# Sixteen conditioning pieces in eight buffers instead of four, and the first squares ahead of the turns

## The chip, the cores and the metric

The kernel runs on one core of a Trainium2 chip. The metric is the device time of one execution in microseconds (us), the median of several runs.

## The reference

One layer of a decoder trunk, for a prompt of 1024 tokens and 8 single-token samples (1032 columns in all, 1024 features), in float32. What matters here is its opening:

```python
mod = jax.nn.silu(c) @ w_ada + b_ada                 # 9 rows of c, w_ada is 1024 x 6144
sh1, sc1, gt1, sh2, sc2, gt2 = jnp.split(mod[:, None, :], 6, axis=-1)
h = rmsnorm(x, norm1_g) * (1.0 + sc1) + sh1
proj = h @ w_in                                      # then conv, RG-LRU, mLSTM and pooling on its parts
x = x + gt1 * (mix @ w_out)
h2 = rmsnorm(x, norm2_g) * (1.0 + sc2) + sh2
x = x + gt2 * (jnp.square(jax.nn.relu(h2 @ w_ff1)) @ w_ff2)
```

`mod` is the conditioning. The normalised `h` of feature tile k needs tile k of `sh1` and of `sc1`, so eight column pairs of `w_ada` must have been worked through before all of `h` is there.

## The kernel before

Activations lie feature-major: 8 tiles of 128 features, 1032 tokens cut into three chunks of 344. Each dense product is made of three matmuls per tile (high by high, low by high, high by low part), so every operand is first split: ScalarE copies it to the high part (`H_hi`, `W_hi`), GpSimd or VectorE subtracts that from the whole (`H_lo`, `W_lo`).

One list, `MIX_ORDER` (line 93), is the order of the first half of the kernel. Each of the engines walks over the whole list and takes the words that concern it, in this order, and waits on semaphores in between; nothing overtakes on an engine. The words of the opening:

- `ADA:i:h`: half h of conditioning pair i (two column tiles of `w_ada`, one piece of 512 KB). TensorE: 8 matmuls (line 2383). ScalarE, for h = 1: copies the result to the one tile ADS (line 1298), when the turn before has been made.
- `ADT:i`: TensorE turns ADS (4 matmuls, line 2397) into a bank that `ADM:i` must have freed. `ADM:i`: VectorE adds the bias and writes MOD (lines 1718, 1720).
- `SQ:c:p`: squares of four tiles of chunk c on ScalarE (line 1279), added up on VectorE (line 1764), two buffers between them. `NS:c`: TensorE spreads the sums over the partitions (line 2403), ScalarE takes the root (line 1258), VectorE the reciprocal (line 1743).
- `N:c:k`: VectorE normalises tile k (lines 1729, 1733), ScalarE adds the shift and makes the high part (lines 1240, 1252, 1253), GpSimd the low part (line 1086). It needs the pairs k // 2 (shift) and 4 + k // 2 (scale), hence `ADA_START = (0, 4, 1, 5, 2, 6, 3, 7)`.
- `W:u`: the split of the weights of unit u, from WR for the first three, high part on ScalarE (line 1235), low part on VectorE for the first two (line 1778). `DK:u:c:a:b`: matmuls of unit u, chunk c, for the tiles a to b, on TensorE (lines 2412 to 2414); it waits for `W:u`'s low part and for each tile's low part.
- `WV:j`: split of V's weights, `WV_hi` on ScalarE and `WV_lo` on VectorE (line 1782); `V:t`: V for 128 tokens (lines 2439 to 2441). It needs all of `WV_lo`.
- `R:n`: ScalarE issues the load of piece n of the later ones.

The pieces are loaded into the four buffers of `RAWW` (`RAW = 4`), piece n into n modulo 4. SyncE issues the first twenty (line 810): it waits (`raw_used`, line 562) until TensorE has used piece n - 4. After some of them it issues other loads (`SP_AFTER`, line 67): W0's weights after piece 5, W1's after piece 7, V's weights and the second chunk of X after piece 15. V's weights take the place of the residual X, which isn't used until much later: `WV_raw` in front, `WV_lo` behind it; `WV_lo` is first written when all sixteen first pieces have been used.

Of the kernel before, what the change touches and what calls it, by code (L numbers as in the profile page):

```python
# [149 lines left out]
D:10:2 HM:1 R:49 R:48 LD:4 EX:2 W:12  # L150
D:11:0 SMB:1 S:2 SX:2 AB:2 NU:2 ADT:18 U:2 CN:2 ADM:18 HN:2 R:50
D:11:1 SMB:2 HM:2 R:52 EX:3 ADA:19:0 S:3 SX:3
D:11:2 SMB:3 AB:3 ADA:19:1 W:13 LDO:0 R:51 NU:3
D:12:0 ADT:19 U:3 HN:3 HM:3 R:53 CN:3 ADM:19 LD:5 ADA:20:0 EX:4 R:55
D:12:1 S:4 SX:4 ADA:20:1 Y:0 R:54 SMC AB:4 NU:4
D:12:2 R:56 U:4 ADT:20 HN:4 W:14 YD:0 R:58 HM:4 LD:6
D:13:0 Y:1 ADM:20 CN:4 ADA:21:0 EX:5 YD:1 R:57
# [129 lines left out]


def build(nc, I, O):
    plan, raw_seq = plan_mix()  # L290
# [23 lines left out]
    with ExitStack() as ctx:  # L314
# [236 lines left out]
        def load_raw(e, n):
            key = raw_seq[n]
            if key[0] == "ADA":
                w = AH * P
                e.dma_start(RAWW[:, n % RAW, :].rearrange("p (e n) -> p e n", e=2),
                            I["WADA"][2 * key[1]:2 * key[1] + 2, :, key[2] * w:(key[2] + 1) * w].rearrange("e p n -> p e n")
                            ).then_inc(raw_in[n % RAW], 16)
# [2333 lines left out]
```

## Time and profile before

| | us |
|---|---|
| median of 3 runs | 1172.3 (1172.24 to 1173.58) |
| profiled execution | 1172.33 |
| its span, first to last instruction | 1170.5 |
| TensorE busy | 1123.7 |
| VectorE, ScalarE, GpSimd busy | 795.6, 470.4, 341.7 |

Times are in us from the start of the span. A row of the timeline gives the start, the time until its last instruction ends, the engine, the line and the operation; in brackets stands the idle time ahead of it and who ended it. "SPq" is SyncE's queue: the time that an issue took, not the transfer. Busy times of TensorE are modelled. PEclk is the clock that was granted to TensorE as a share of 2.4 GHz.

### The profile page before, as it was taken

How to read it: one execution, taken by the hardware profiler on the slowest of the kernel's cores; microseconds unless marked ns; L12 is line 12 of the kernel's file. 1: busy time of each engine (PE TensorE's matmuls, PEld its weight loads, DVE VectorE, ACT ScalarE, POOL GpSimd, SP SyncE). 2: the span in 40 equal slices, each digit the busy share in tenths (PEclk: the TensorE clock that was granted, in tenths of full speed). 3: DMA queues.
4: the chain of work that ended last, by engine and by line, in shares of the span. 5: the costliest groups of instructions: out<-in, count | busy, mean ns of one | idle time of the engine just before them, and what ended most of it. 6: DMA issues, size and time to landing. Idle time of an engine off the chain costs nothing.

```text
span 1170.5 us, 19691 instructions
## 1 busy us (share of the span) xinstructions
PE 1123.7 (96%) x7237; PEld 1075.4 (92%) x7237; DVE 795.6 (68%) x1327; ACT 470.4 (40%) x774; POOL 341.7 (29%) x273
## 2 busy tenths in 40 slices
PE   4899999999989999999999999999999999999997
PEld 2688888888978999899999999999999999999996
DVE  4472455489775434778678879778778787788546
ACT  5452355555456343642233332332432433433431
POOL 1133011201425357764022032122231231231352
PEclk9799999999989999999999999999999999999998
DMA  9812523566623822111111111202202102111104
GB/s 316 311 66 82 142 91 126 171 186 225 187 79 122 270 75 72 54 55 37 37 36 55 56 36 60 66 18 72 67 9 80 59 18 78 47 53 55 37 1 145
DMA packets 67846, 109.85 MB, mean 94 GB/s; under 512 B 6435, under 2 KB 42567, under 8 KB 67399
## 3 DMA queue, kind: packets, MB, share of 16 engines
q1 hardware_dynamic: 57574, 84.88, 21.9%
q10 hardware_dynamic: 10208, 24.12, 6.5%
q8 instruction: 41, 0.67, 0.2%
q14 instruction: 23, 0.18, 0.0%
HBM read 96.81 MB, written 12.18 MB: 93 GB/s over the span
## 4 chain that ended last, share of the span: by engine, by line
PE 81%; DVE 11%; ACT 3%; issue 1%; POOL 1%; DMA 1%; SPq 0%; ACTq 0%; POOLq 0%; DVEq 0%
PE D L2412 7%; PE D L2414 6%; PE D L2413 6%; PE D L2596 6%; PE D L2598 5%; PE D L2597 5%; PE X L2598 5%; PE X L2596 5%; PE X L2597 5%; PE X L2668 5%; PE X L2670 5%; PE X L2669 5%; PE D L2668 2%; PE D L2670 2%; PE D L2669 2%
## 5 line engine op out<-in xcount | busy, mean ns | idle before, releaser
L2412 PE MATMUL D<-H_hi,W_hi 128*128 128x344 f32 x472 | 159.1, 337 | 6.9 <-POOL H_lo L1086 6.1
L2414 PE MATMUL D<-H_hi,W_lo 128*128 128x344 f32 x472 | 152.1, 322 | 0.0
L2413 PE MATMUL D<-H_lo,W_hi 128*128 128x344 f32 x472 | 152.1, 322 | 0.0
L1086 POOL TENSOR_TENSOR Y_lo<-FU,Y_hi 128x344 fp32r<-128x344 f32 (+3 forms) x84 | 100.1, 1195 | 153.7 <-ACT Y_hi L1522 87.6
L1081 POOL TENSOR_TENSOR W_lo<-RAWW,W_hi 128x1024 fp32r<-128x1024 f32 x25 | 61.3, 2452 | 178.8 <-ACT W_hi L1235 178.5
L2412 PEld LDWEIGHTS D<-H_hi,W_hi 128*128 128x128 f32 x472 | 90.1, 191 | 17.7 <-issue 11.8
L1086 POOL TENSOR_TENSOR Y_lo<-EY,Y_hi 128x344 fp32r<-128x344 f32 (+1 forms) x24 | 38.3, 1597 | 216.3 <-ACT Y_hi L1522 144.5
L2413 PEld LDWEIGHTS D<-H_lo,W_hi 128*128 128x128 f32 x472 | 90.1, 191 | 0.6 <-issue 0.2
L2414 PEld LDWEIGHTS D<-H_hi,W_lo 128*128 128x128 f32 x472 | 89.8, 190 | 0.0
L2220 DVE SCALAR_TENSOR_TENSOR X<-X,MOD 128x344 f32<-128x344 f32 (+1 forms) x138 | 75.6, 566 | 9.3 <-PE X L2670 9.2
L2668 PE MATMUL X<-Y_hi,W_hi 128*128 128x344 f32 x252 | 80.7, 320 | 0.0
L2669 PE MATMUL X<-Y_lo,W_hi 128*128 128x344 f32 x252 | 80.6, 320 | 0.0
L2670 PE MATMUL X<-Y_hi,W_lo 128*128 128x344 f32 x252 | 80.5, 319 | 0.0
L2022 DVE SCALAR_TENSOR_TENSOR X<-D,MOD,X 128x344 f32<-128x344 f32 (+1 forms) x72 | 41.3, 573 | 45.5 <-PE D L2598 24.7
L2412 PE MATMUL D<-Y_hi,W_hi 128*128 128x344 f32 x192 | 62.0, 323 | 1.5 <-POOL W_lo L1081 1.5
L1098 POOL TENSOR_TENSOR SS<-SS,SQ 128x344 f32<-128x344 f32 x45 | 43.4, 964 | 65.8 <-ACT SQ L1431 40.5
L1086 POOL TENSOR_TENSOR Y_lo<-KEPT,Y_hi 128x344 fp32r<-128x344 f32 x24 | 26.3, 1097 | 121.5 <-ACT Y_hi L1522 121.5
L2414 PE MATMUL D<-Y_hi,W_lo 128*128 128x344 f32 x192 | 61.3, 320 | 0.0
L2413 PE MATMUL D<-Y_lo,W_hi 128*128 128x344 f32 x192 | 61.3, 319 | 0.0
L1557 ACT ACTIVATE W_hi<-RAWW 128x1024 fp32r<-128x1024 f32 x30 | 31.7, 1058 | 63.9 <-PE X L2670 55.3
L1086 POOL TENSOR_TENSOR H_lo<-FU,H_hi 128x344 fp32r<-128x344 f32 (+2 forms) x33 | 29.6, 916 | 71.4 <-ACT FU L1253 57.8
L2670 PEld LDWEIGHTS X<-Y_hi,W_lo 128*128 128x128 f32 x252 | 47.4, 188 | 0.0
(417 smaller groups left out, 3434.8 us busy)
## 6 DMA issues: line engine op xcount, KB each, us to landing
RAWW<-in_W SPq DMA_DIRECT2D x76, 512.0 KB, 3.6
RAWW<-in_WADA ACTq DMA_DIRECT2D x28, 512.0 KB, 4.1
RAWW<-in_WADA SPq DMA_DIRECT2D x20, 512.0 KB, 6.5
RAWW<-in_W ACTq DMA_DIRECT2D x18, 512.0 KB, 3.7
X0T<-in_x SPq DMA_DIRECT2D x3, 1376.0 KB, 12.9
out_y<-OUTN SPq DMA_DIRECT2D x24, 172.0 KB
X<-in_x SPq DMA_DIRECT2D x8, 344.0 KB, 5.5
NM<-nm_d SPq DMA_DIRECT2D x8, 256.0 KB, 5.4
```

Of the source, the lines that this page charges most:

```text
L1081: nc.gpsimd.tensor_tensor(lo_v, RAWW[:, raw, :] if src is None else src[:], hi_v.bitcast(F32), ALU.subtract).then_inc(w_lo_ready, 1)
L1086: nc.gpsimd.tensor_tensor(lo_v, fu_v, hi_v.bitcast(F32), ALU.subtract).then_inc(lo_ready, 1)
L2220: V.scalar_tensor_tensor(out=X[:, m, c * CH:c * CH + w], in0=ps[:, 0:w], scalar=MOD[:, 5 * KT + m, 0:1], in1=X[:, m, c * CH:c * CH + w], o ...
L2412: T.matmul(out, w_h, hi[:, kt, a:b], start=(kt == 0), stop=False)
L2413: T.matmul(out, w_h, lo[:, kt, a:b], start=False, stop=False)
L2414: one = T.matmul(out, w_l, hi[:, kt, a:b], start=False, stop=(kt == KT - 1))
L2596: T.matmul(out, w_h, hi(kt), start=(kt == 0 and not onto), stop=False, skip_group_check=onto)
L2597: T.matmul(out, w_h, lo(kt), start=False, stop=False, skip_group_check=onto)
L2598: one = T.matmul(out, w_l, hi(kt), start=False, stop=(kt == n - 1), skip_group_check=onto)
L2668: T.matmul(bank[:, 0:CH], w_hi[:, a:a + P], h, start=(start and k == 0), stop=False, skip_group_check=onto)
L2669: T.matmul(bank[:, 0:CH], w_hi[:, a:a + P], l, start=False, stop=False, skip_group_check=onto)
L2670: one = T.matmul(bank[:, 0:CH], w_lo[:, a:a + P], h, start=False, stop=(stop and k == 1), skip_group_check=onto)
```

## The change

The first sixteen pieces get eight buffers. Of each eight, the first four use `RAWW` and the others four spare tiles, three where `WV_lo` will be and one in slot 15, which isn't used then. SyncE waits for the use of piece n - 8 instead of n - 4. The order of the loads and what is issued after which stay as they are. The later pieces have indices lower by eight, so they lie in the same buffers modulo four; this is why every `R:n` in the list changes.

In the list, `SQ:0:1` goes from behind `ADA:4:1` to right behind `SQ:0:0`; `NS:0` goes ahead of `ADA:1:0` and `ADT:4`; `W:0` goes from ahead of `N:0:0` to behind `ADM:1`; `DK:0:0:0:2` goes ahead of `ADA:2:0` and `ADT:5`; `W:1` goes behind `ADM:5`. From `N:0:2` on the order is the same.

```diff
-ADA_FIRST = 2 * len(ADA_START)
+ADA_EARLY = [("ADA", i, h) for i in ADA_START for h in range(2)]
-N_SP_RAW = 2 * len(ADA_START) + RAW
+SPARE = 4
+SPARE_PIECES = [k for n, k in enumerate(ADA_EARLY) if n % (RAW + SPARE) >= RAW]
-R0 = NADA - N_EARLY_W
+R0 = NADA - N_EARLY_W - len(SPARE_PIECES)
...
-ADA:0:0 ADA:0:1 SQ:0:0 ADA:4:0 ADT:0 ADM:0 ADA:4:1 SQ:0:1 ADA:1:0 ADT:4 ADM:4 NS:0 ADA:1:1 W:0 N:0:0 N:0:1 ADA:5:0 ADT:1 ADM:1
-ADA:5:1 W:1 ADA:2:0 ADT:5 ADM:5 DK:0:0:0:2 N:0:2 N:0:3 ADA:2:1 DK:1:0:0:2 ADA:6:0 ADT:2 ADM:2 ADA:6:1 DK:0:0:2:4
+ADA:0:0 ADA:0:1 SQ:0:0 SQ:0:1 ADA:4:0 ADT:0 ADM:0 ADA:4:1 NS:0 ADA:1:0 ADT:4 ADM:4 ADA:1:1 N:0:0 N:0:1 ADA:5:0 ADT:1 ADM:1 W:0 ADA:5:1
+DK:0:0:0:2 ADA:2:0 ADT:5 ADM:5 W:1 N:0:2 N:0:3 ADA:2:1 DK:1:0:0:2 ADA:6:0 ADT:2 ADM:2 ADA:6:1 DK:0:0:2:4
...
+        SPARE_RAW = [at(f"SPARE{r}", [P, KT * P], rX + KT * VCOLS * 4 + r * KT * P * 4 if r < SPARE - 1 else slot[15]) for r in range(SPARE)]
...
         def raw_wait(e, key):
+            if key in SPARE_PIECES:
+                n = SPARE_PIECES.index(key)
+                e.wait_ge(spare_in[n % SPARE], 16 * (n // SPARE + 1))
+                return SPARE_RAW[n % SPARE][:]
             n = raw_at[key]
             e.wait_ge(raw_in[n % RAW], 16 * (n // RAW + 1))
-            return n % RAW
+            return RAWW[:, n % RAW, :]
...
-            for n in range(N_SP_RAW):
-                if n >= RAW:
-                    raw_used(sp, n - RAW)
-                load_raw(sp, n)
+            for n, key in enumerate(sp_raws):
+                if key in SPARE_PIECES:
+                    k = SPARE_PIECES.index(key)
+                    if k >= SPARE:
+                        used(sp, SPARE_PIECES[k - SPARE])
+                    load_piece(sp, key, SPARE_RAW[k % SPARE][:], spare_in[k % SPARE])
+                else:
+                    if raw_at[key] >= RAW:
+                        raw_used(sp, raw_at[key] - RAW)
+                    load_raw(sp, raw_at[key])
```

## Rows read from the trace of the kernel before

**Rows 1.** The page, part 1: busy time, share of the span, instructions.
```profile
PE 1123.7 (96%) x7237; PEld 1075.4 (92%) x7237; DVE 795.6 (68%) x1327; ACT 470.4 (40%) x774; POOL 341.7 (29%) x273
```

**Rows 2.** Timeline of TensorE, the first V product.
```profile
51.66 0.69 PE L2439 MATMUL X<-WV_hi,H_hi 128*128 128x392 f32 x1 [0.50 <-DVE WV_lo L1782]
```

**Rows 3.** Waits of TensorE, 10 to 60 us: total, times, longest.
```profile
PE X L2383 <- DMA RAWW<-in_WADA: 13.5, 5, 10.6
PE X L2397 <- ACT ADS L1298: 3.4, 3, 1.7
```

**Rows 4.** SyncE's issues, and the sixteenth piece: KB, us from issue to landing.
```profile
18.52 16.84 SPq L555 DMA_DIRECT2D RAWW<-in_WADA  x8
...
34.99 0.37 SPq L555 DMA_DIRECT2D RAWW<-in_WADA  x1
...
RAWW<-in_WADA SPq DMA_DIRECT2D x1, 512.0 KB, 5.7
```

**Rows 5.** Stretches: us, busy (x) of PE, PEld, DVE, ACT, POOL; PEclk, DMA, GB/s.
```profile
20.00:25.00 5.00, 3.89 (x30) 1.30 (x29) 3.24 (x2) 2.03 (x4) 0.00 (x0) 1.00 1.00 382
...
30.00:35.00 5.00, 5.00 (x37) 2.76 (x37) 1.74 (x5) 1.70 (x4) 1.79 (x2) 0.72 0.40 111
```

**Rows 6.** Timeline of TensorE, 17 to 34 us.
```profile
17.38 1.08 PE L2383 MATMUL X<-RAWW,CTX 128*32 128x256 f32 x8 [1.14 <-DMA RAWW<-in_WADA]
...
19.52 1.51 PE L2403 MATMUL X<-SS,ONE 128*128 128x344 f32 x2
...
22.70 0.61 PE L2397 MATMUL X<-SEL,ADS 128*128 128x9 f32 x4
...
25.20 0.64 PE L2383 MATMUL X<-RAWW,CTX 128*32 128x256 f32 x8 [1.31 <-DMA RAWW<-in_WADA]
27.57 1.03 PE L2397 MATMUL X<-SEL,ADS 128*128 128x9 f32 x4 [1.73 <-ACT ADS L1298]
28.44 0.63 PE L2412 MATMUL D<-H_hi,W_hi 128*128 128x344 f32 x1
...
30.44 1.08 PE L2383 MATMUL X<-RAWW,CTX 128*32 128x256 f32 x8
...
33.74 0.61 PE L2397 MATMUL X<-SEL,ADS 128*128 128x9 f32 x4
```

**Rows 7.** Timeline of VectorE, 17 to 31 us.
```profile
17.26 2.21 DVE L1764 TENSOR_TENSOR SS<-SS,SQ 128x344 f32<-128x344 f32 x4 [0.89 <-ACT SQ L1279]
...
21.73 2.31 DVE L1743 RECIPROCAL X<-SS 128x344 f32<-128x344 f32 x1 [1.82 <-ACT SS L1258]
24.07 1.23 DVE L1778 TENSOR_TENSOR W_lo<-WR,W_hi 128x1024 fp32r<-128x1024 f32 x1
25.21 1.05 DVE L1729 SCALAR_TENSOR_TENSOR FU<-X0T,MOD,X 128x344 f32<-128x344 f32 x2
...
28.56 1.25 DVE L1778 TENSOR_TENSOR W_lo<-WR,W_hi 128x1024 fp32r<-128x1024 f32 x1 [1.78 <-ACT W_hi L1235]
...
30.15 1.06 DVE L1729 SCALAR_TENSOR_TENSOR FU<-X0T,MOD,X 128x344 f32<-128x344 f32 x2
```

**Rows 8.** Timeline of ScalarE, 22 to 33 us.
```profile
22.46 1.05 ACT L1235 ACTIVATE W_hi<-WR 128x1024 fp32r<-128x1024 f32 x1
25.81 0.58 ACT L1252 ACTIVATE H_hi<-FU,MOD 128x344 fp32r<-128x344 f32 x1 [2.30 <-DVE FU L1729]
...
27.15 0.36 ACT L1298 ACTIVATE ADS<-X 128x256 f32<-128x256 f32 x1
...
32.09 0.36 ACT L1298 ACTIVATE ADS<-X 128x256 f32<-128x256 f32 x1
```

**Rows 9.** Stretches, TensorE alone: us, busy (x), PEclk, DMA, GB/s.
```profile
25.80:29.20 3.40, 1.67 (x11) 0.52 0.99 368
29.20:32.60 3.40, 3.40 (x17) 0.50 0.19 70
...
53.10:56.50 3.40, 3.40 (x12) 0.50 1.05 394
```

More of the change, by code:

```diff
@@ L111 @@
 DK:1:1:4:5
-R:20 ADA:8:1 DK:0:1:5:6
+R:12 ADA:8:1 DK:0:1:5:6
 SQ:2:0 DK:1:1:5:6
@@ L118 @@
 D:0:1 ADT:8
-D:1:1 V:2 NS:2 N:2:8 N:2:0 R:21 N:2:1 N:2:2 V:3 N:2:3 N:2:4 N:2:5 N:2:6 V:4 N:2:7 ADM:8 DK:0:2:0:8
+D:1:1 V:2 NS:2 N:2:8 N:2:0 R:13 N:2:1 N:2:2 V:3 N:2:3 N:2:4 N:2:5 N:2:6 V:4 N:2:7 ADM:8 DK:0:2:0:8
 W:2 V:5
-D:0:2 R:22 DK:1:2:0:8
-ADA:9:0 ADA:9:1 R:23 V:6 V:7 W:3 V:8 R:25 ADT:9
+D:0:2 R:14 DK:1:2:0:8
+ADA:9:0 ADA:9:1 R:15 V:6 V:7 W:3 V:8 R:17 ADT:9
 D:1:2 ADM:9 ADA:10:0 G1 ADA:10:1
-D:2:0 ADT:10 R:24
-D:2:1 ADM:10 R:26 G2
-D:2:2 R:28 W:4 G3 ADA:11:0 R:27 R:29
+D:2:0 ADT:10 R:16
+D:2:1 ADM:10 R:18 G2
+D:2:2 R:20 W:4 G3 ADA:11:0 R:19 R:21
 D:3:0 ADA:11:1 G4
-D:3:1 R:31 ADT:11 LRUC:0
+D:3:1 R:23 ADT:11 LRUC:0
 D:3:2 ADM:11 W:5 ADA:12:0
-D:4:0 R:30 ADA:12:1 LRUG:0 R:32 LRUA:0
+D:4:0 R:22 ADA:12:1 LRUG:0 R:24 LRUA:0
 D:4:1 LRUM:0
-D:4:2 R:34 W:6
-D:5:0 ADT:12 ADM:12 ADA:13:0 ADA:13:1 R:33 LRUC:1
+D:4:2 R:26 W:6
+D:5:0 ADT:12 ADM:12 ADA:13:0 ADA:13:1 R:25 LRUC:1
 D:5:1
-D:5:2 ADT:13 R:35 ADM:13 ADA:14:0 LRUG:1 ADA:14:1
-D:6:0 R:37 W:7 ADT:14 LRUA:1 R:36 R:38 ADM:14
+D:5:2 ADT:13 R:27 ADM:13 ADA:14:0 LRUG:1 ADA:14:1
+D:6:0 R:29 W:7 ADT:14 LRUA:1 R:28 R:30 ADM:14
 D:6:1 LRUM:1
-D:6:2 R:40 ADA:15:0
+D:6:2 R:32 ADA:15:0
 D:7:0
-D:7:1 W:8 ADA:15:1 LRUC:2 R:39
+D:7:1 W:8 ADA:15:1 LRUC:2 R:31
 D:7:2 ADT:15 LRUG:2 LRUA:2
-D:8:0 R:41 ADM:15 ADA:16:0 W:9
-D:8:1 R:43
-D:8:2 R:42 ADA:16:1 R:44 W:10 LD:0 SMA TS TSD ADT:16 LRUM:2
+D:8:0 R:33 ADM:15 ADA:16:0 W:9
+D:8:1 R:35
+D:8:2 R:34 ADA:16:1 R:36 W:10 LD:0 SMA TS TSD ADT:16 LRUM:2
 D:9:0
-D:9:1 R:46 R:45 LD:1 ADM:16 EX:0 ADA:17:0 S:0 SX:0 ADA:17:1 W:11 AB:0 R:47
+D:9:1 R:38 R:37 LD:1 ADM:16 EX:0 ADA:17:0 S:0 SX:0 ADA:17:1 W:11 AB:0 R:39
 D:9:2 ADT:17 U:0 NU:0 HN:0 CN:0 ADM:17 HM:0 EX:1 ADA:18:0 SMK S:1 SX:1 SMB:0
@@ L149 @@
 D:10:1 LD:3 AB:1 NU:1 ADA:18:1 U:1 CN:1 HN:1
[L150 to L157, printed above, removed]
+D:10:2 HM:1 R:41 R:40 LD:4 EX:2 W:12
+D:11:0 SMB:1 S:2 SX:2 AB:2 NU:2 ADT:18 U:2 CN:2 ADM:18 HN:2 R:42
+D:11:1 SMB:2 HM:2 R:44 EX:3 ADA:19:0 S:3 SX:3
+D:11:2 SMB:3 AB:3 ADA:19:1 W:13 LDO:0 R:43 NU:3
+D:12:0 ADT:19 U:3 HN:3 HM:3 R:45 CN:3 ADM:19 LD:5 ADA:20:0 EX:4 R:47
+D:12:1 S:4 SX:4 ADA:20:1 Y:0 R:46 SMC AB:4 NU:4
+D:12:2 R:48 U:4 ADT:20 HN:4 W:14 YD:0 R:50 HM:4 LD:6
+D:13:0 Y:1 ADM:20 CN:4 ADA:21:0 EX:5 YD:1 R:49
 D:13:1 S:5 ADA:21:1 POOLV:0 YS POOLS:0 POOLD:0 SX:5 W:15 YSD AB:5 NU:5 HN:5 HM:5
-D:13:2 ADT:21 R:59 U:5 CN:5
+D:13:2 ADT:21 R:51 U:5 CN:5
 D:14:0 Y:2 ADM:21 EX:6 YD:2
-D:14:1 ADA:22:0 S:6 SX:6 R:61 AB:6 ADA:22:1 Y:3 POOLV:1
-D:14:2 POOL:0:0 POOLS:1 NU:6 YD:3 R:60 POOLY:0:0 POOL:0:1 ADT:22 POOLY:0:1 HN:6 LD:7 POOL:0:2 POOLD:1 POOLY:0:2 ADM:22
-    HM:6
-D:15:0 U:6 Y:4 POOL:1:0 R:62 CN:6 POOLY:1:0 ADA:23:0 EX:7 POOL:1:1 W:16 R:64 YD:4
-D:15:1 POOLY:1:1 S:7 SX:7 POOL:1:2 POOLY:1:2 ADA:23:1 R:63
+D:14:1 ADA:22:0 S:6 SX:6 R:53 AB:6 ADA:22:1 Y:3 POOLV:1
+D:14:2 POOL:0:0 POOLS:1 NU:6 YD:3 R:52 POOLY:0:0 POOL:0:1 ADT:22 POOLY:0:1 HN:6 LD:7 POOL:0:2 POOLD:1 POOLY:0:2 ADM:22
+    HM:6
+D:15:0 U:6 Y:4 POOL:1:0 R:54 CN:6 POOLY:1:0 ADA:23:0 EX:7 POOL:1:1 W:16 R:56 YD:4
+D:15:1 POOLY:1:1 S:7 SX:7 POOL:1:2 POOLY:1:2 ADA:23:1 R:55
 D:15:2 Y:5 YD:5 AB:7 NU:7 ADT:23 HN:7
-D:16:0 R:65 HM:7 Y:6 U:7 YD:6 CN:7 ADM:23
+D:16:0 R:57 HM:7 Y:6 U:7 YD:6 CN:7 ADM:23
 D:16:1 Y:7 W:17 YD:7
@@ L173, in plan_mix @@
 def plan_mix():
-    raws = [("ADA", i, h) for i in ADA_START for h in range(2)]
+    raws = [k for k in ADA_EARLY if k not in SPARE_PIECES]
     pairs = [i for i in range(NPAIR) if i not in ADA_START]
     early, pairs = pairs[:2], pairs[2:]
-    raws += [("ADA", i, h) for i in early for h in range(2)]
+    early = [("ADA", i, h) for i in early for h in range(2)]
+    raws += early
     for u in range(3, N_MIX):
@@ L185, in plan_mix @@
         out.append((name, *(int(a) for a in args)))
-    return out, raws
+    return out, raws, ADA_EARLY + early
 AUX = ["X0", "X1", "X2", "X3", "X4"]
@@ L289, in build @@
 def build(nc, I, O):
-    plan, raw_seq = plan_mix()
+    plan, raw_seq, sp_raws = plan_mix()
     use = bank_uses(plan)
@@ L298, in build @@
     P_FF = P_MIX + P_NORM
-    assert len(raw_seq) == N_MIX - N_EARLY_W + NADA
+    assert len(raw_seq) == N_MIX + R0
     raw_seq += [("W", u) for u in range(N_MIX, N_MIX + RAW)]
     raw_at = {k: n for n, k in enumerate(raw_seq)}
-    ADA_ORDER = [k[1] for k in raw_seq if k[0] == "ADA" and k[2] == 0]
+    ADA_ORDER = list(ADA_START) + [k[1] for k in raw_seq if k[0] == "ADA" and k[2] == 0 and k[1] not in ADA_START]
     SHIFTED = ((1, 3, 5, 7, KT), (KT - 2, KT - 1, KT))
@@ L478, in build @@
         raw_in = [sem(f"raw{r}_in") for r in range(RAW)]
+        spare_in = [sem(f"spare{r}_in") for r in range(SPARE)]
         w_hi_ready, w_lo_ready = sem("w_hi_ready"), sem("w_lo_ready")
@@ L549, in in_unit, with load_piece @@
             return IN_FIRST[UNIT_KIND[u][0]] + UNIT_KIND[u][1] if u < N_MIX else u
+        def load_piece(e, key, dst, landed):
+            w = AH * P
+            e.dma_start(dst.rearrange("p (e n) -> p e n", e=2),
+                        I["WADA"][2 * key[1]:2 * key[1] + 2, :, key[2] * w:(key[2] + 1) * w].rearrange("e p n -> p e n")
+                        ).then_inc(landed, 16)
         def load_raw(e, n):
@@ L553, in load_raw @@
             if key[0] == "ADA":
[L554 to L557, printed above, removed]
+                load_piece(e, key, RAWW[:, n % RAW, :], raw_in[n % RAW])
             else:
@@ L560, in load_raw, with used @@
                 e.dma_start(RAWW[:, n % RAW, :], I["W"][in_unit(u)]).then_inc(raw_in[n % RAW], 16)
-        def raw_used(e, n):
-            key = raw_seq[n]
+        def used(e, key):
             if key[0] == "W":
@@ L570, in raw_used @@
                 e.wait_ge(ada_half, ADA_ORDER.index(key[1]) + 1)
+        def raw_used(e, n):
+            used(e, raw_seq[n])
         def mod_ready(e):
@@ L2383, in ada @@
                     one = T.matmul(ps[32 * j:32 * j + 32, 0:2 * P], CTX[:, k:k + 32],
-                                   RAWW[:, raw, :].rearrange("p (e k n) -> p e k n", e=2, k=AH)[:, :, j, :],
+                                   raw.rearrange("p (e k n) -> p e k n", e=2, k=AH)[:, :, j, :],
                                    start=(half == 0), stop=(half == 1), tile_position=(0, 32 * j))
```

## The prediction

> **What bounds the kernel now.** I read the page's first part before anything else: TensorE is busy for 96% of the span [rows 1], so outside the opening nearly everything is a chain of matmuls and a change to the opening is worth what it shifts the first long run of them. Its end in time is the first V product. It starts at 51.66, and what ended the wait before it was V's low half of the weights on VectorE [rows 2]. From there the work runs on in one order, so I ask only how far that point moves, and what clock TensorE has when it gets there.
>
> Next I read the waits of TensorE between 10 and 60 us. Five waits for conditioning pieces sum to 13.5 us, but 10.6 us of this is the wait for the very first one, which no buffer count can shorten. The other four are 2.9 us together. Three waits for ScalarE's copy into ADS are 3.4 us [rows 3]. Then the queue of transfers: SyncE issues the ninth to sixteenth piece one by one from 18.52 to 35.4 us, each when TensorE has given a buffer back; the sixteenth, issued at 34.99, lands 5.7 us later, at 40.7 [rows 4]. The queue is full where pieces are outstanding (382 GB/s) and nearly empty at 30 to 35 us (111 GB/s) [rows 5]. So the hole in the transfers is there. But the last time TensorE waits for a piece is before 25.20 [rows 6]: after that the pieces are there when their turn comes.
>
> What sets the order after 19 us is a chain over four engines: the squares' sums end on VectorE at 19.47, TensorE spreads them (19.52, 1.51 us), ScalarE takes the root, VectorE the reciprocal (21.73, 2.31 us), then it makes the first low weights (24.07), then normalises the first two tiles (25.21). ScalarE splits those from 25.81 and only then copies ADS (27.15), on which TensorE's turn for pair 5 waits (27.57); the products of unit 0 follow at 28.44 [rows 6 to 8].
>
> **Part 1, eight buffers.** The first four pieces are issued as before. The next four no longer wait. The first sixteen pieces, W0 and W1 then follow each other at the full rate. Before, the ninth piece landed at 25.2, where TensorE's wait for it ended [rows 6], out of a queue at full rate. At that rate a piece of 0.524 MB takes 1.37 us; seven more give 34.8, less the 1.1 us by which the fifth had come late (the wait before 17.38): the sixteenth lands at 33.7, 7.0 us earlier. The pieces up to the thirteenth gain only about that 1.1 us, because their stretch was already at full rate. What this is worth on TensorE is bounded by its waits: 2.9 us at most, and nothing at the least. I take the lower end: 1.14 us of them sit before 17.38, while the sums that everything needs end at 19.47, and 1.31 sit before 25.20, after which TensorE waits again, 1.73 us, for ADS. V's weights and the next part of X are issued behind the sixteenth piece and land earlier too; they weren't what was waited for [rows 2]. From piece R:12 on the indices are lower by eight, so every buffer is the same one modulo four, and nothing changes.
>
> **Part 2, the squares ahead of the turns.** ScalarE squares all eight tiles in one go. The second four sums started 0.89 us late, plus 0.2 us of a modulation between; the end moves from 19.47 to 18.36, 1.1 us earlier [rows 7]. Spread 18.4 to 19.9, root to 20.5, reciprocal 20.6 to 22.9. On TensorE ADA:1:0 and the turn of pair 4 now stand behind the spread; pieces of 1.0 us each put that turn at 21.9, so its modulation follows the reciprocal (0.4 us), and the first two tiles are normalised from 23.4, 1.8 us earlier than 25.21. This is the change's gain, with W0's low part (1.1 us) out of its way.
>
> **Part 3, what the new order puts in the path.** W:0 moved behind N:0:0, N:0:1 and ADM:1 on ScalarE and VectorE. Before, ScalarE made W0's high part in the reciprocal's shadow. Now: tiles split on ScalarE until 25.4 (25.81 to 27.2 shifted by 1.8), high part 1.05 us until 26.4, low part 1.25 us until 27.7. DK:0:0:0:2, the first six matmuls, moved ahead of ADA:2:0 and ADT:5, and it needs that low part. TensorE has ADA:5:0, ADT:1 and ADA:5:1 done by 24.4 (the turn starts at 23.2, when the modulation of pair 4 has freed its bank; 0.6 us each) and then stands for 3.3 us, with ADA:2:0 and ADT:5 queued behind although piece 8 has landed. At 27.75 the six matmuls run. The clock: it was granted at the lower of its two levels, 1.2 GHz, from just before 26 to 32.6, after two idle spells of 1.3 and 1.7 us [rows 6, 9]. The new idle spell is longer and lies in the same place, so I take the lower level again: 2.0 us for the six (28.44 to 30.44), 1.0 for ADA:2:0 (30.44), 1.0 for the turn (27.57) [rows 6]. ADT:5 ends at 31.75 instead of 28.6.
>
> VectorE then: modulation 0.4 us (what lies between W1's low part and N:0:2 in [rows 7]) to 32.2; W1's low part, which before was made ahead of that modulation, 1.2 us to 33.4; then N:0:2, at 33.4 instead of 30.15. ScalarE's next ADS copy came 1.94 us after that start [rows 7, 8]: 35.35 to 35.7. The turn of pair 2 runs at 35.75 instead of 33.74: **2.0 us later**. The shift is less than the 3.2 of VectorE because TensorE was itself the last to arrive there before. From this word on both orders are the same, the steps are a closed chain of turns, modulations, normalising and splitting with no transfer in it, and the first V product begins at 53.7 instead of 51.66. If the clock were not lowered in that stall, the same steps take 0.6 us for a piece (25.20) and for a turn (22.70) and half of 2.0 for the six matmuls, and the shift is 0.2 us. That is the other end of this term; I take 2.0, since the idle spell is longer than those after which it fell.
>
> **Part 4, the clock over the V product.** Before, the lower level covered V's first 4.8 us (until about 56.5), which cost 2.4 us. Where it ends after the shift depends on when the level rises after the gap; from a level already back at 53.7 (saves 2.4 us, of which the sums for the second part of X, made behind V's low weights, allow 2.1) to one 6.8 us long (costs 1.0 more; 6.8 is the length of the other spell, 25.8 to 32.6). The middle of -2.1 and +1.0 is -0.5. Sum: 2.0 - 0.5 = +1.5 us.
>
> The profiled execution took 1172.33 us with a span of 1170.5, the median is 1172.3; the sum on either gives **1173.8 us**. A difference of 0.2% (2.3 us) is about what a measurement of this kernel can tell from no change; +1.5 is inside it.
>
> Two rules of the Trainium skill stand beside this. "Trainium Kernel Development and Optimization", section Best Practices, says to double-buffer so that transfers overlap compute. By it alone, deeper buffers should pay; [rows 3] leave 2.9 us for it at most, the first rival. "TensorE: Matmul & The Clock Gate", section Step-by-step: what each phase is for, says that matmuls stay in program order and only weight loads are pulled ahead. It speaks against the change: a DK that waits holds the ready ADA behind it. The rows agree as far as they go: its matmuls stand there in the order of the list [rows 6]. By it the shift is the 2.0 us above; if ADA:2:0 could overtake, it would be 0.
>
> **Rivals.** (a) The transfers decide: each wait for a piece that lies after the first goes and passes down. 1172.3 - 2.9 = 1169.4 us. For it: the hole at 30 to 35 us and the 1.8 us that the first normalised tile gains. Against it: the waits lie ahead of others. In this case unit 0's products don't stall, or the clock stays high in their stall. Chance 0.13. If the landing of the sixteenth piece itself set the end, it would be 7.0 us, 1165.3; no wait for it exists after 25.20, so I give this 0.03.
> (b) The stall at DK:0:0:0:2 costs more: the lower clock level, fallen in the stall, lasts past 36 us because TensorE stands again for W1 and ADS (32.7 to 33.4 and 35.2 to 35.7). Six more matmuls and a piece at the lower level add 0.6 to 1.5 us, and V then runs at the lower level for another 1.0. 2.0 + 1.0 + 1.0 = +4.0: 1176.3 us. It decides from the point at which the level is still low at 33.5, when DK:1:0:0:2 starts. Chance 0.27.
> (c) It doesn't do what it says: SyncE's issue is held up by a full queue, so the pieces come as before. Time from order alone, again +1.5: it can't be told apart by time. It is inside the forecast, chance 0.57 together.
>
> **Range and chances.** From 1169.6 (most of rival a) to 1176.6 (rival b). Faster by over 0.2%: 0.13 (a and its larger form, less their part inside 0.2%). Slower: 0.30, all of b and the upper edge of the forecast. Same: 0.57.
>
> **What would show it.** Right: the sixteenth piece lands at 33 to 35; the sums end near 18.4; TensorE waits about 3 us for W0's low part ahead of the first DK; the turn of pair 2 starts near 35.7; V's first product near 53.7. Wrong: pair 2's turn before 34, or V's product before 51.7, would mean that the stall is shorter than worked out or the clock stayed up; a span changed by more than V's first product moved would mean that the clock or a later stage did it.

## The result, and the profile after

The changed kernel takes **1178.8 us** (median of 5 runs, 1177.66 to 1180.8), the kernel before in the same sitting 1172.9 (5 runs, 1172.24 to 1174.89). The ratio is **1.0050, 95% interval 1.0035 to 1.0064**: slower by 5.9 us. The forecast was 1173.8, in a range of 1169.6 to 1176.6; the time lies above it. The profiled execution of the kernel after took 1179.43 us, with a span of 1177.6 (before 1172.33 and 1170.5).

The page of the kernel after, part 1; it answers to [rows 1]:

```profile
PE 1128.2 (96%) x7237; PEld 1077.0 (91%) x7237; DVE 796.4 (68%) x1327; ACT 470.5 (40%) x774; POOL 341.2 (29%) x273
```

Not one instruction was added, yet TensorE is busy for 4.5 us more than in [rows 1]: the same matmuls took longer. So at least a part of the loss is clock and not waiting.

Waits of TensorE's matmuls, 10 to 60 us, kernel after (total, times, longest); they answer to [rows 3]:

```profile
PE X L2402 <- DMA RAWW<-in_WADA: 10.7, 3, 10.2
PE D L2431 <- DVE W_lo L1797: 3.1, 2, 2.3
```

The waits for pieces after the first are 0.5 us instead of 2.9. The buffers alone do as much (0.4 in e1 below), but so does the order in four buffers (0.4 in e8 below), and a second trace of the kernel before has only 1.1. The new entry is the wait for low weights.

Timeline of TensorE, kernel after, 18 to 57 us (start, length, line, operation, idle time before and who ended it); it answers to [rows 2] and [rows 6]:

```profile
18.24 1.51 PE L2422 MATMUL X<-SS,ONE 128*128 128x344 f32 x2 [2.33 <-DVE SS L1783]
19.69 1.08 PE L2402 MATMUL X<-SPARE,CTX 128*32 128x256 f32 x8
20.70 1.02 PE L2416 MATMUL X<-SEL,ADS 128*128 128x9 f32 x4
...
27.88 0.66 PE L2431 MATMUL D<-H_hi,W_hi 128*128 128x344 f32 x1 [2.32 <-DVE W_lo L1797]
...
30.91 1.02 PE L2416 MATMUL X<-SEL,ADS 128*128 128x9 f32 x4
...
33.68 0.66 PE L2431 MATMUL D<-H_hi,W_hi 128*128 128x344 f32 x1 [0.73 <-DVE W_lo L1797]
...
36.71 1.02 PE L2416 MATMUL X<-SEL,ADS 128*128 128x9 f32 x4
...
40.28 0.49 PE L2433 MATMUL D<-H_hi,W_lo 128*128 128x344 f32 x1
...
42.75 0.31 PE L2433 MATMUL D<-H_hi,W_lo 128*128 128x344 f32 x1
...
56.96 0.44 PE L2458 MATMUL X<-WV_hi,H_hi 128*128 128x392 f32 x1 [0.75 <-DVE WV_lo L1801]
...
61.54 0.85 PE L2422 MATMUL X<-SS,ONE 128*128 128x344 f32 x2
```

The reader is to see three things. TensorE stands at 27.88 for W0's low part, and behind it the piece and the turn that were ready. The turn of pair 2 starts at 36.71 (before 33.74), the first V product at 56.96 (before 51.66). And up to 42 us every short matmul has the longer of its two durations: 0.49 against 0.31 for line 2433, 1.02 against 0.61 for a turn [rows 6].

Stretches of TensorE, kernel after (stretch, us, busy (x), PEclk, DMA, GB/s):

```profile
22.40:25.80 3.40, 3.16 (x24) 1.00 1.06 388
...
33.70:42.10 8.40, 8.40 (x42) 1.00 1.03 382
42.10:52.10 10.00, 6.60 (x53) 1.00 0.93 333
52.30:55.70 3.40, 3.02 (x11) 0.51 0.02 5
56.00:61.00 5.00, 4.25 (x25) 1.00 0.01 2
```

These rows have a trap. PEclk reads 1.00 from 22.4 to 42.1, but the matmuls there have the durations of 1.2 GHz. The trace holds a record only when the level changes, and a stretch ahead of the first record is printed as 1.00. The first record here is a rise, at 42.1. In the kernel before the first record is a rise at 22.5, and its piece at 17.38 takes 1.08 us and the one at 25.20 takes 0.64 [rows 6]; the 1.00 of [rows 5] is right from 22.5 on only. Ahead of the first record, read the durations.

From 42 us on the steps run as before, but later; V, which ran its first 4.9 us at 1.2 GHz before (51.66 to 56.6 [rows 9]), has 2.4 GHz from its start. The first matmul after V's group is at 61.54, before at 58.28: +3.26. This stays within 0.1 us up to 230 us. Then it grows. Timeline of TensorE at 249 us, after, and at 244 us, before: the first turns of keys of an attention chunk, which wait for `VB` read back from memory:

```profile
248.71 0.55 PE L2522 MATMUL X<-IDN,K 96*128 96x96 f32 x4 [1.79 <-DMA VB<-v_d]
```

```profile
244.27 0.55 PE L2503 MATMUL X<-IDN,K 96*128 96x96 f32 x4 [1.05 <-DMA VB<-v_d]
```

There the shift goes to +4.4; after this longer wait the recorded level is at 1.2 GHz from 250.3 to 253.7, where before it wasn't, and it becomes +5.6 (at 340 us). A wait for `W_lo` at 390.52 that was not there before brings it to +6.7 at 400 us, and the end is at +7.1 in this pair of executions.

### The profile page after: what moved, and what is told of

Its sections match the earlier page's. It is cut to its first block, busy times and chain, and to the rows that moved or that the text cites. A ratio compares the mean times of both kernels' runs of the same rounds, so it can differ in the third digit from the quotient of the medians.

```text
span 1177.6 us, 19691 instructions
## 1 busy us (share of the span) xinstructions
PE 1128.2 (96%) x7237; PEld 1077.0 (91%) x7237; DVE 796.4 (68%) x1327; ACT 470.5 (40%) x774; POOL 341.2 (29%) x273
## 4 chain that ended last, share of the span: by engine, by line
PE 79%; DVE 11%; ACT 3%; DMA 2%; issue 1%; POOL 1%; SPq 1%; DVEq 0%; POOLq 0%; ACTq 0%
PE D L2431 6%; PE D L2433 6%; PE D L2432 6%; PE D L2615 6%; PE D L2617 5%; PE D L2616 5%; PE X L2617 5%; PE X L2615 5%; PE X L2616 5%; PE X L2687 5%; PE X L2689 5%; PE X L2688 5%; PE D L2687 2%; PE D L2689 2%; PE D L2688 2%
## 5 line engine op out<-in xcount | busy, mean ns | idle before, releaser
L2041 DVE SCALAR_TENSOR_TENSOR X<-D,MOD,X 128x344 f32<-128x344 f32 (+1 forms) x72 | 41.3, 573 | 44.9 <-PE D L2617 24.7
L1576 ACT ACTIVATE W_hi<-RAWW 128x1024 fp32r<-128x1024 f32 x30 | 31.7, 1058 | 64.0 <-PE X L2689 55.3
L2239 DVE SCALAR_TENSOR_TENSOR X<-D,MOD,X 128x344 f32<-128x344 f32 (+1 forms) x78 | 43.0, 571 | 6.5 <-PE D L2689 5.4
```

The lines of the kernel that those rows point to most:

```text
L2239: V.scalar_tensor_tensor(out=X[:, m, c * CH:c * CH + w], in0=ps[:, 0:w], scalar=MOD[:, 5 * KT + m, 0:1], in1=X[:, m, c * CH:c * CH + w], o ...
```

## Experiments

The opening can be read to a tenth of a microsecond in a trace, the whole time only to about 2 us. So each run is given as a ratio, with the kernel before timed beside it, and as three marks from its trace: the time from which the trace first records 2.4 GHz (R), the start of pair 2's turn (T), and the start of the first V product (V). The first piece starts between 9.89 and 10.65 us in these traces, so differences of the marks under about 0.5 us mean little. Before: R 22.5, T 33.74, V 51.66. After: R 42.1, T 36.71, V 56.96.

**1. The buffers alone, and the order alone.** The first kernel has the eight buffers and the old list; the second is the kernel before with the two new lines of the list.

```diff
 # e1: the kernel after, with the list's lines of before
-ADA:0:0 ADA:0:1 SQ:0:0 SQ:0:1 ADA:4:0 ...
-DK:0:0:0:2 ADA:2:0 ADT:5 ADM:5 W:1 N:0:2 ...
+ADA:0:0 ADA:0:1 SQ:0:0 ADA:4:0 ...
+ADA:5:1 W:1 ADA:2:0 ADT:5 ADM:5 DK:0:0:0:2 N:0:2 ...
```

> Eight buffers as in the changed kernel, the list's first two lines as in the kernel before. Order theory (the new order costs 2 us by itself and leaves TensorE at its lower clock level up to 42 us, which costs 3 more): the first V product starts at 51 to 52 us as before (51.66), the sixteenth piece lands near 34 instead of 40.7, time 1171.5 to 1173.5. Buffer theory (the deeper queue of transfers slows something in the opening or in the early loads): the first V product starts at 54 or later and the time is 1175 or more. If the waits of 2.9 us for pieces were on the path: V at 49 to 50 and 1170.

Ratio 0.9999 (0.9988 to 1.0009). R 22.4, T 33.43, V 51.33. Timeline of TensorE of this kernel:

```profile
27.05 1.02 PE L2416 MATMUL X<-SEL,ADS 128*128 128x9 f32 x4 [2.79 <-ACT ADS L1317]
```

Its wait for ADS is 2.79 us where [rows 6] has 1.73 behind a wait of 1.31 for a piece. The piece was there earlier, and nearly all of that went into the next wait. The time shows neither a cost nor a gain of the buffers.

> Four buffers as in the kernel before, the list's first two lines as in the changed kernel. Order theory: as the changed kernel, 1177 to 1180, first V product at 55 to 58 us, TensorE standing 2 to 3 us for W0's low part before its first dense product near 27.9. Buffer theory: 1172 to 1174, V at 52 to 54.

Ratio 1.0023 (1.0013 to 1.0034). R 37.1, T 36.71, V 54.76. The stall is the same with four buffers:

```profile
27.88 0.66 PE L2412 MATMUL D<-H_hi,W_hi 128*128 128x344 f32 x1 [2.32 <-DVE W_lo L1778]
```

So the stall and the late rise belong to the order, and the buffers alone cost nothing. The time leaves a gap: 1.0023 is less than half of the 1.0050 of the kernel after, whose interval starts at 1.0035, where this one has ended. Another timing of the kernel after (1.0046, from 1.0029, experiment 5) overlaps with this one. No run here shows whether the eight buffers add a loss once the order is the new one; at the marks they don't (T is 36.71 in both traces).

**2. One word of the order at a time, from the kernel after.** e3 puts the first matmuls back behind the turn (and W:1 ahead of it), and keeps the early squares and the late W:0. e4 puts W:0 back alone.

```diff
 # e3
-DK:0:0:0:2 ADA:2:0 ADT:5 ADM:5 W:1 N:0:2
+W:1 ADA:2:0 ADT:5 ADM:5 DK:0:0:0:2 N:0:2
 # e4
-ADA:1:1 N:0:0 N:0:1 ADA:5:0 ADT:1 ADM:1 W:0 ADA:5:1
+ADA:1:1 W:0 N:0:0 N:0:1 ADA:5:0 ADT:1 ADM:1 ADA:5:1
```

> The changed kernel with DK:0:0:0:2 back behind ADM:5 and W:1 back ahead of ADA:2:0; W:0 stays behind ADM:1 and the squares stay early. If the place of DK (the blocked turn of pair 5) is the cause: ADT:5 ends near 26.5 to 27.5, N:0:2 starts near 28.5 to 29.5, V at 50 to 51.5 and 1170.5 to 1172.5. If W:0's late split is the cause whatever stands behind it: V at 53 or later, 1175 or more.

Ratio 0.9983 (0.9968 to 0.9999), a median of 1172.31 beside 1173.84: the loss is gone, and the kernel is just faster than the one before. R 33.1, T 33.39, V 51.19. Timeline of TensorE of e3:

```profile
26.18 1.02 PE L2416 MATMUL X<-SEL,ADS 128*128 128x9 f32 x4
27.54 0.66 PE L2431 MATMUL D<-H_hi,W_hi 128*128 128x344 f32 x1 [0.34 <-DVE W_lo L1797]
```

The turn of pair 5 starts at 26.18 instead of 30.91, and the first matmuls run at 27.54, no later than in the kernel after: what stood in front of the turn waited for nothing but itself.

> The changed kernel with W:0 back ahead of N:0:0, DK:0:0:0:2 and W:1 as changed. Then W0's low part is ready by 24.3 and the first dense product can run at 26.5 to 27. If the late split of W0 is the cause: ADT:5 ends near 30, V at 52 to 53.5 unless the clock level stays low, 1173 to 1175. If the place of DK and W:1 is what costs: ADT:5 at 29.5 to 30.5, W1's low part still behind it, V at 54 to 56, 1176 to 1178.

Ratio 1.0032 (1.0018 to 1.0045). R 46.5, T 37.27, V 57.92. Timeline of TensorE of e4:

```profile
28.40 0.63 PE L2431 MATMUL D<-H_hi,W_hi 128*128 128x344 f32 x1 [2.67 <-POOL H_lo L1105]
```

The same word now waits for the first tile's low part and starts no earlier. VectorE makes W0's low part at 24.47, ahead of the normalising of the two tiles, and that starts at 25.61 instead of 23.21; the low part of the first tile comes later by this much. The expectation had the first matmuls at 26.5 to 27 and V at 56 at the latest: it left this out. So W:0's old place doesn't take the stall away.

**3. The two halves of that word, from the kernel before.** e9 moves only the first matmuls ahead of the turn; e10 moves only W:1 behind it.

```diff
 # e9
-ADA:5:1 W:1 ADA:2:0 ADT:5 ADM:5 DK:0:0:0:2 N:0:2
+ADA:5:1 W:1 DK:0:0:0:2 ADA:2:0 ADT:5 ADM:5 N:0:2
 # e10
+ADA:5:1 ADA:2:0 ADT:5 ADM:5 DK:0:0:0:2 W:1 N:0:2
```

> The kernel before with one edit: DK:0:0:0:2 goes ahead of ADA:2:0, ADT:5 and ADM:5. Squares, W:0, W:1 and the four buffers as before. If the place of DK is the cause: TensorE stands 3 to 4 us from 24 to 28 for the first tiles' low parts, ADT:5 ends at 31 to 32.5, N:0:2 starts at 32 to 33.5, the turn of pair 2 at 35.5 to 37, the first V product at 54 to 57, time 1176 to 1179. If it needs the early squares or the late W:0 beside it: V at 51.5 to 53, 1173 to 1175.

Ratio 1.0017 (0.9996 to 1.0039), with single runs from 1171.49 to 1184.78. R 30.6, T 34.06, V 51.97: V is 0.3 us later, where in the kernel after it is 5.3 us later. So I took a second trace of the same kernel:

> The ninth experiment's kernel (DK early, nothing else) again. Its first trace had the level back at 30.6 us and V at 51.97. If that was one lucky execution: the level stays low until 36 or later, V at 54 to 57. If the early squares and the late W:0 are needed for the long stay at the low level: V at 51.5 to 53 again.

1177.83 us, R 40.4, T 35.49, V 55.57. Stretches of TensorE, the first trace and then the second (columns as above):

```profile
22.40:30.40 8.00, 4.87 (x30) 1.00 0.69 242
```

```profile
22.40:30.40 8.00, 4.87 (x26) 1.00 0.60 219
33.00:40.20 7.20, 7.20 (x40) 1.00 0.64 196
```

The code is the same, and up to the stall the two agree: the first matmuls start at 27.62 and 27.50, behind the same wait of 3.13 us for a tile's low part. One execution then gets 2.4 GHz at 30.6, the other at 40.4, and V starts 3.6 us apart. V itself then runs at 2.4 GHz in the first and at 1.2 GHz until 60.9 in the second, so that the first matmul behind V's group starts at 56.55 and at 62.37: 5.8 of the 6.3 us between the two spans. That is what the clock alone was worth here.

> The kernel before with one edit: W:1 goes behind ADM:5 and DK:0:0:0:2, which stay where they were. W1's low part is then made at 29 to 30.5 instead of 28.56 to 29.8, in ADM:5's wake: N:0:2 starts at 30.2 to 30.7, V at 51.5 to 52.3, 1173 to 1175 (no cost of its own). If the place of W:1 is the cause of the late N:0:2: N:0:2 after 32, V after 53.5, 1176 or more.

Ratio 1.0015 (0.9999 to 1.0031); R 22.4, T 33.39, V 51.44. In the order of before, W:1's place does nothing in the opening. Behind an early DK it is another matter: the normalising of the third tile (N:0:2) starts at 31.98 in e15, where W1's low part is made ahead of the stalled turn, and at 33.54 in the kernel after, and DK:1:0:0:2, which waits for that low part, starts at 32.46 and at 33.68. Counted from the first matmuls (27.50 and 27.88), that is 0.8 us later, and the turn of pair 2 is 0.8 us later too. So some 0.8 of the 3.0 us at T go with W:1's place. The two kernels differ in more than W:1, and no run moves W:1 alone with DK early, so this is an estimate.

**4. The clock by itself.** If the lower level makes half the loss, matmuls that do nothing, set where TensorE stands anyway, should give it back with the stall left in. e5 is the kernel after with five of them ahead of NS:0 and five ahead of the first matmuls.

```diff
+FILL:5 DK:0:0:0:2 ADA:2:0 ADT:5 ADM:5 W:1 N:0:2
...
+elif k == "FILL":
+    for _ in range(s[1]):
+        T.matmul(DB[2][:, 0:P], ONE[:], ONE[:], start=True, stop=True)
```

> The changed kernel with ten products of ONE by ONE (128 columns) added on TensorE, into a bank that nothing uses yet: five ahead of NS:0, where it stands 2.3 us for the sums, five ahead of DK:0:0:0:2, where it stands 2.3 us for W0's low part. They take away no wait. Clock theory (3 of the 5.3 us at the first V product are the lower clock level up to 42 us): the level rises before 33 us, the turn of pair 2 starts at 35 to 36 instead of 36.7, the first V product at 52.5 to 54.5 instead of 56.96, time 1173.5 to 1176. If the order alone is the cause: V at 56 to 58 and 1178 to 1180.

R 18.4, T 35.13, V 53.21. Timeline of TensorE of e5:

```profile
27.33 0.43 PE L2431 MATMUL D<-H_hi,W_hi 128*128 128x344 f32 x1 [2.30 <-DVE W_lo L1797]
...
53.21 0.45 PE L2461 MATMUL X<-WV_hi,H_hi 128*128 128x392 f32 x1 [0.71 <-DVE WV_lo L1801]
```

The stall of 2.3 us is as long as before, and V starts 3.75 us earlier than in the kernel after, 0.5 from the forecast's 53.7. The first matmul behind V's group starts at 57.78, against 61.54 in the kernel after and 58.28 in the kernel before: in this trace the opening's loss is gone with the stall left in. But the span gets only 1.8 of these 3.8 us, and the ratio is 1.0031 (1.0009 to 1.0053), which overlaps with that of the kernel after: the times don't show the gain. This trace waits 3.07 us for `EX` at 238.44 (before 0.72, at 236.61) and has 1.2 GHz from 236.9 to 243.7. A second trace, to see whether the late waits come with the fills:

> The fifth experiment's kernel again. Its first trace had V at 53.21 but a time of 1177.6. If the added products really lift the level: V at 52.5 to 54.5 again, and what is above 1174 lies after 230 us. If the added products help only in some executions: V after 56.

1177.54 us, R 18.8, T 33.71, V 54.05, behind V's group 58.63; waits for `EX` of 1.94 and for `VB` of 1.97 us. The opening's gain is there in both, and so are long late waits, not the same ones.

**5. Does the opening of the kernel after always look so?** Two more traces of it, and one more of the kernel before:

> The changed kernel once more, on the chip of these runs. If the lower clock level up to about 42 us belongs to this order and not to one execution: it rises after 36 us again, V at 55 to 58, 1176.5 to 1179.5. If it was a matter of that execution alone: level rises at 22 to 33 us, V at 53 to 54.5.

> The changed kernel, a third trace. The level was back at 42.1 and at 45.7 us in the first two, V at 56.96 and 57.08. The same order should give a rise after 36 us and V at 55 to 58; a rise before 34 and V near 53.7 would mean that it is left to the execution.

> The kernel before, another execution. If its level rises at 22 to 23 us whatever the execution: low again from 26 to 33, first V product at 51 to 52. If the moment hangs on the execution: a rise after 26, V at 52 to 55, and the times of this kernel are spread by it.

The kernel after: ratio 1.0046 (1.0029 to 1.0064), R 45.7, T 36.53, V 57.08; then 1176.8 us, R 37.7, T 37.08, V 55.24. The kernel before: 1173.26 us, R 31.7, T 33.16, V 51.68. Its level rose nine microseconds later than in the first trace and V began at the same time, which is neither of the two expectations. The reason is in the stretches of TensorE of the first trace (stretch, us, busy (x), PEclk, DMA, GB/s):

```profile
22.50:25.90 3.40, 2.02 (x24) 1.00 0.99 362
25.90:32.80 6.90, 5.23 (x23) 0.51 0.62 215
```

The early rise lasted 3.4 us, into waits for a piece and for ADS, and from 25.9 to 32.8 the level was low again. From the steps ahead of T on, both traces have 2.4 GHz from nearly the same time, 32.8 and 31.7. It is so in e1 and e10 too; for these three the table gives the second rise as well. The last columns are the start of the first matmul behind V's group (B) and the span, less that of the first trace of before. In order of R:

| kernel | first matmuls ahead of the turn | R | T | V | B | span, less before's |
|---|---|---|---|---|---|---|
| e1, buffers alone | no | 22.4, 32.7 | 33.43 | 51.33 | 58.09 | +1.8 |
| e10, W:1 alone | no | 22.4, 32.6 | 33.39 | 51.44 | 58.12 | +1.7 |
| before | no | 22.5, 32.8 | 33.74 | 51.66 | 58.28 | 0 |
| e9, DK alone | yes | 30.6 | 34.06 | 51.97 | 56.55 | -0.8 |
| before, again | no | 31.7 | 33.16 | 51.68 | 57.80 | +1.0 |
| e3, DK back | no | 33.1 | 33.39 | 51.19 | 55.77 | -1.8 |
| e2, order alone | yes | 37.1 | 36.71 | 54.76 | 59.34 | +9.8 |
| after, third | yes | 37.7 | 37.08 | 55.24 | 59.82 | +4.5 |
| e15, DK alone, again | yes | 40.4 | 35.49 | 55.57 | 62.37 | +5.5 |
| after | yes | 42.1 | 36.71 | 56.96 | 61.54 | +7.1 |
| after, again | yes | 45.7 | 36.53 | 57.08 | 61.65 | +5.7 |
| e4, W:0 back | yes | 46.5 | 37.27 | 57.92 | 62.50 | +6.0 |

All six traces in which the level is back by 33.1 start V by 52.0. Past that V goes with R, from 54.8 to 57.9. All but one of the traces with the stall lie in the lower half; none without it does. The third trace of the kernel after, with a rise at 37.7, loses only 1.5 us up to B, where the other two lose 3.3 and 3.4.

**6. Versions that use this.** e8 is e3's list in four buffers. e6 and e12 add fills to e3, e7 to the kernel before; all start with 16 ahead of the first piece, where TensorE stands for 10 us, and have some in later gaps.

```diff
 # e6: e3, with
+FILL:16 ADA:0:0 ... FILL:5 NS:0 ... FILL:1 DK:0:0:0:2 ... FILL:5 WV:0 DK:0:0:6:7
 # e12: e3, with
+FILL:16 ADA:0:0 ... FILL:10 NS:0 ... FILL:2 ADT:1 ... FILL:2 ADA:2:0 ... FILL:1 DK:0:0:0:2 ... FILL:5 WV:0 DK:0:0:6:7 ... FILL:3 (ahead of V)
 # e7: before, with
+FILL:16 ADA:0:0 ... FILL:3 ADT:5 ... FILL:5 WV:0 DK:0:0:6:7
```

> The third experiment's order in the four buffers of the kernel before. If the eight buffers bring something once the order is right: TensorE waits 1 to 3 us for pieces, V at 52 to 54, 1173 to 1175.5. If they bring nothing: V at 51 to 52, 1171 to 1173, as the third experiment.

> The third experiment's kernel (DK behind ADM:5) with such products added: sixteen ahead of the first piece, where TensorE stands until 10 us, five ahead of NS:0, one ahead of the first dense product, five ahead of the last gap before DK:0:0:6:7. Clock theory: upper level from before 15 us, V's first product at 49 to 51 us and at the upper level, time 1167.5 to 1170.5. If the clock there is worth nothing: V at 51 and 1171 to 1173.5. If the added work is in the way: V after 52 and 1174 or more.

> The kernel before with sixteen such products ahead of the first piece, three ahead of ADT:5, five ahead of the last gap. Clock theory: upper level through the opening but for short falls, V's first product at 49.5 to 51.5 us and at the upper level, time 1169 to 1171.5. If the clock there is worth nothing: 1172.5 to 1175.

> As the sixth experiment, with more products in the gaps: ten ahead of NS:0, two ahead of ADT:1, two ahead of ADA:2:0, three ahead of the first V product. Clock theory: the level doesn't fall between 12 and 25 us, the first V product at 48.5 to 50, 1169.5 to 1171.5. If the chain over ScalarE and VectorE alone sets the end by now: V at 49.8 to 50.5 whatever the level, 1170.5 to 1172.5.

| kernel | ratio (95%) | R | T | V |
|---|---|---|---|---|
| e8, e3 in four buffers | 0.9993 (0.9976 to 1.0009) | 31.4 | 32.78 | 50.56 |
| e6, e3 and fills | 0.9988 (0.9970 to 1.0006) | 9.2, 29.7 | 31.49 | 50.09 |
| e7, before and fills | 0.9981 (0.9966 to 0.9996) | 7.3, 31.2 | 32.76 | 51.35 |
| e12, e3 and more fills | 0.9974 (0.9955 to 0.9994) | 9.4, 29.9 | 31.59 | 50.06 |

e3, e7 and e12 beat both kernels; their intervals lie below 1 (e3's by 0.0001 only), and below the 1.0035 of the kernel after. Among the three nothing can be told apart. e6 started V within its forecast, but its median of 1171.54 is above the forecast's 1170.5, and its interval takes in 1. e12's added fills kept the level up until 26.5 instead of e6's 19.4, and V starts at the same time, 50.06 against 50.09: as its second expectation has it, more clock brings nothing there. With four buffers e3's list starts V even a little earlier than with eight.

## Why the prediction was wrong, by its own steps

**Part 1, the buffers: right.** It took them at nothing, with 2.9 us as the other end. The trace of after has the sixteenth piece issued last, just ahead of 26.0, and landed 7.4 us later: 33.4 (forecast 33.7). e1 measures 0.9999. Rival (a), that the transfers decide, fell with it: in e1 the waits of [rows 3] behind the first went down from 2.9 to 0.4 us and V moved by 0.3. The Trainium skill ("Trainium Kernel Development and Optimization", Best Practices) has double-buffering pay by overlap; here the overlap was gained and e1 shows no time for it. Rival (c) fell too: the pieces do come early.

**Part 2, the squares: right.** Timeline of VectorE, kernel after; it answers to [rows 7]:

```profile
15.98 2.21 DVE L1783 TENSOR_TENSOR SS<-SS,SQ 128x344 f32<-128x344 f32 x4 [0.16 <-ACT SQ L1298]
...
23.21 1.06 DVE L1748 SCALAR_TENSOR_TENSOR FU<-X0T,MOD,X 128x344 f32<-128x344 f32 x2
...
26.31 1.52 DVE L1797 TENSOR_TENSOR W_lo<-WR,W_hi 128x1024 fp32r<-128x1024 f32 x1 [1.52 <-ACT W_hi L1254]
...
32.40 1.23 DVE L1797 TENSOR_TENSOR W_lo<-WR,W_hi 128x1024 fp32r<-128x1024 f32 x1
33.54 1.05 DVE L1748 SCALAR_TENSOR_TENSOR FU<-X0T,MOD,X 128x344 f32<-128x344 f32 x2
```

The sums end at 18.19 (forecast 18.36), the first tiles are normalised from 23.21 (forecast 23.4, before 25.21).

**Part 3, the order: the path right, one assumption in it wrong.** W0's low part is ready at 27.83 (27.7), the first matmuls start at 27.88 (27.75), N:0:2 at 33.54 (33.4). TensorE does keep the order of the list, as the Trainium skill says ("TensorE: Matmul & The Clock Gate", Step-by-step: what each phase is for): the turn of pair 5 stands behind the stall in all nine traces of the five kernels that have it. e3 shows it by undoing: with the first matmuls and W:1 back in their old places the opening is no slower than before. The assumption is the clock ahead of the stall: Part 3 counted 0.6 us each for ADA:5:0, ADT:1 and ADA:5:1, from a kernel whose level had risen at 22.5, and had TensorE free at 24.4, to stand for 3.3 us. Here each took 1.0 us, TensorE was free at 25.56 and stood for 2.32. The end of the stall doesn't depend on this, since W0's low part sets it.

**The step that failed** is "from this word on both orders are the same [...] the turn of pair 2 runs at 35.75: 2.0 us later" together with Part 4. It took the level to be back at 2.4 GHz from 32.6, as in the kernel before, and so left TensorE waiting for ADS (35.35 to 35.7). With the lower level lasting, TensorE itself is last: six matmuls from 33.68 take 2.0 us instead of 1.0, the piece 1.0 instead of 0.6, and the turn starts at 36.71, although ADS is there at 35.84. That is +3.0 instead of +2.0. From there to V the steps take 20.25 us (36.71 to 56.96) where before they took 17.92; that is +2.3, which the prediction had at nothing. Of this, 2.2 us lie between the turns of pair 2 and pair 6 (36.71 to 41.71, before 33.74 to 36.57), where every matmul ran at 1.2 GHz. The other traces give the same two figures: 20.1 in e15, with R at 40.4, and 17.9 in e9 and 17.8 in e3, with R by 33.1. In the third trace of the kernel after, R at 37.7, it is 18.2: the first term is there in each trace of this kernel, the second isn't.

This was rival (b), given 0.27. Its point of decision was right: at 33.68 the level was still low. Its sizes were not. It had +1.0 for the steps up to V, where +1.0 and +2.3 came, and +1.0 for V itself, where V gained 2.0 (5.30 at its start, 3.26 behind it), next to the end of -2.1 that Part 4 had worked out. 2.0 + 1.0 + 2.3 - 2.0 = **+3.3**, instead of rival (b)'s 4.0 and the forecast's 1.5.

Under it lies a misreading: that the level would *fall* in the new stall, from 2.4 GHz, and come back as before. In the kernel before it did fall, at 25.9, but ahead of 22.5 its matmuls have the durations of 1.2 GHz too. In the kernel after nothing fell in the stall; the level didn't rise until 42.1. The Trainium skill ("TensorE: Matmul & The Clock Gate", Part 1: The HAM clock gate) says that the throttled state is the default, and activity releases it. The traces agree with the first half: where no fills stand ahead of the first piece, the first pieces take 1.08 us, and a later one at 2.4 GHz takes 0.64. For the second half they have the fills of e5, which brought R from 42.1 to 18.4, and against a simple reading of it the 8.4 us without a gap at 1.2 GHz. The prediction had the row against it, 1.08 us for the piece at 17.38 beside 0.64 at 25.20 [rows 6], and used both durations without asking why they differ.

**What the forecast had no term for** is the rest. In the first pair of traces it is 7.1 - 3.3 = 3.8 us, all behind 230 us; in the other two traces of the kernel after 2.3 and 3.0. But the second trace of the kernel before has 1.5 too, and e1 and e10, which change nothing in the opening, have 2.0 and 1.9; e5 has 5.8, and e2, the new order in four buffers, 8.7, the most of all. It comes in waits for `EX` and `VB` of 0.7 to 3.1 us, and in falls of the level behind the longer of them. The kernel before's own profiled execution is at the low end of this spread. Three traces of after against two of before make it 3.0 against 0.7 on average. Whether the order has a part in that, or so few executions happened to fall so, stays open: no run here separates it.

What also stays open is why the level rises when it does. The table makes it likely that the stall brings a late rise: six of its seven traces with the stall have it after 33.1 us, and none of the six without it (with e8) does. That it doesn't settle it is shown by e9 and e15, one code with rises ten microseconds apart. That a late rise, not the stall itself, costs the larger part of the opening's loss is shown at V and B by e5, e9 and e15. For the whole time it isn't shown: the intervals of e5 and of the kernel after overlap, and the interval of e9, the stall in the old order, takes in 1.

## What to carry to other kernels

An engine that works in program order should meet no word ahead of a ready one if that word waits for a longer chain: the wait is handed to everything behind it, and the ready word here led to the next turn of the closed chain, whose steps the whole opening follows. Work out what a deeper buffer is worth from the wait that would come next, as e1's 2.79 us shows, not from the hole in the transfers. And when a short stretch is to be costed, take the durations of TensorE's instructions in it as the witness for its clock, and cost the stretch at both levels to its end, not until the level rose in the kernel before.

## What was not expected of the hardware

- TensorE can be busy without a gap in the trace and stay at 1.2 GHz: 8.4 of 8.4 us in the kernel after (33.7 to 42.1), 11.8 of 11.8 in its second trace (33.7 to 45.5), 7.2 of 7.2 in e15. What ran there were pieces, turns and matmuls of 128x344.
- Matmuls that compute nothing can move the rise: with ten of them, put where TensorE stood anyway, the kernel after started V at 53.21 and 54.05 us in two traces, without them at 55.24 to 57.08 in three. Its time didn't fall clear of the noise.
- A first rise nine microseconds earlier was worth nothing: R 22.5 and 31.7 in two traces of the kernel before, V at 51.66 and 51.68. The level had fallen again at 25.9 and came back at 32.8.
- Two executions of one code (e9 and e15) lay 6.3 us apart in their spans, 5.8 of them from the opening, where one had 2.4 GHz from 30.6 and the other from 40.4.
- The waits around 240 us differ between executions by microseconds: 0.72 to 3.07 us for `EX`, which VectorE makes, and up to 2.00 us for `VB`, which is read back from memory.
